# Dense products of a fused two-block transformer kernel: one plain fp32 matmul in place of three on split operands, and a ring of ten places

## The reference

```python
def first_block(...):            # 2 layers
    for l in range(DEPTH):
        mix = token_mixing(...)  # z = x @ w_in; pooled, sparse-attention and memory branches,
                                 # each times w_br, weighed by sigmoid(x @ w_gate), summed, @ w_out
        x = layer_norm(DN_ALPHA * x + mix, ln1_g[l], ln1_b[l])
        ffn = moe(...)           # 16 experts, 2 per token: (silu(x @ w1) * (x @ w3)) @ w2
        x = layer_norm(DN_ALPHA * x + ffn, ln2_g[l], ln2_b[l])

def _layer(...):                 # second block, 2 layers
    z = rms(x) @ w_in            # then window attention, forget-gate attention, mLSTM
    x = x + concat([ya, yb, yc]) @ w_out
    u = rms(x, norm2) @ w_ff1
    return x + square(relu(u)) @ w_ff2
```

## Time and profile before

| | |
|---|---|
| median of 3 executions | 2056.72 us (2053.87 to 2058.24) |
| the profiled execution's own time | 2056.15 us |
| its span, first to last instruction | 2053.5 us |
| PE busy | 1757.6 us |
| DVE busy | 773.7 us |
| ACT busy | 643.4 us |
| mean granted TensorE clock | 0.912 |

### The profile page before, as it was taken

One profiled execution on the slowest core, in us unless ns is written; L12 is line 12 of the kernel. 1 busy time (PEld: TensorE's weight loads), 2 busy tenths in 40 slices (PEclk: granted clock), 3 DMA queues, 4 the chain that ended last, 5 costly groups with the idle time before them and its releaser, 6 DMA issues.

```text
span 2053.5 us, 22089 instructions
## 1 busy us (share of the span) xinstructions
PE 1757.6 (86%) x9214; PEld 1290.8 (63%) x9214; DVE 773.7 (38%) x1476; ACT 643.4 (31%) x1041; POOL 29.5 (1%) x49
## 2 busy tenths in 40 slices
PE   5898987798897998987798895867899988588999
PEld 4768886443334777885443332855499977447997
DVE  3545443200104446343200103634255545525554
ACT  2425531110002435521110003443244443514442
POOL 4000000000000000000000000000000000000000
PEclk8999998799998999998799997875899999669999
DMA  8343445499997453445499995430155546003553
GB/s 237 98 144 118 139 153 203 148 387 386 386 387 244 124 163 107 142 163 186 153 386 386 387 386 201 147 123 0 41 185 185 186 136 199 13 21 103 191 189 112
DMA packets 233278, 392.67 MB, mean 191 GB/s; under 512 B 7124, under 2 KB 97280, under 8 KB 232784
## 3 DMA queue, kind: packets, MB, share of 16 engines
q1 hardware_dynamic: 229760, 380.30, 53.9%
q0 software_dynamic: 3264, 9.61, 1.5%
q10 hardware_dynamic: 144, 1.24, 0.2%
HBM read 390.07 MB, written 1.05 MB: 190 GB/s over the span
## 4 chain that ended last, share of the span: by engine, by line
PE 71%; DVE 9%; DMA 7%; SPq 6%; ACT 5%; issue 2%; DVEq 0%; ACTq 0%
PE psum L503 68%; SPq L2034 6%; DMA ring_sb<-in_w 4%; PE psum L629 2%; DMA ring_sb<-in_w_in 1%; ACT ring_rounded L1092 1%; DVE ring_rounded L1434 1%; DMA ring_sb<-in_w_out 1%; PE psum L548 1%; ACT region_sb L1118 1%; DVE x_sb L1545 0%; ACT xT_hi_rounded L1317 0%; DVE x_sb L1543 0%; DVE region_sb L1818 0%; DVE region_sb L1821 0%
## 5 line engine op out<-in xcount | busy, mean ns | idle before, releaser
L503 PE MATMUL psum<-ring_sb,region_sb 128*64 128x512 f32 (+1 forms) x1728 | 431.8, 602 | 44.3 <-DMA ring_sb<-in_w 34.5
L1434 DVE TENSOR_TENSOR ring_rounded<-ring_sb,ring_rounded 128x2048 fp32r<-128x2048 f32 (+4 forms) x152 | 321.5, 2130 | 259.0 <-ACT ring_rounded L1092 259.0
L503 PE MATMUL psum<-xT_hi_rounded,ring_rounded 128*128 128x256 f32 x1920 | 356.1, 287 | 0.0
L503 PEld LDWEIGHTS psum<-ring_sb,region_sb 128*64 128x64 f32 (+1 forms) x1728 | 151.5, 144 | 308.4 <-issue 289.6
L1092 ACT ACTIVATE ring_rounded<-ring_sb 128x2048 fp32r<-128x2048 f32 (+4 forms) x152 | 268.1, 1781 | 225.3 <-PE psum L503 143.2
L503 PE MATMUL psum<-ring_rounded,xT_hi_rounded 128*128 128x384 f32 (+4 forms) x960 | 280.1, 369 | 44.8 <-DVE ring_rounded L1434 25.2
L503 PE MATMUL psum<-xT_lo_rounded,ring_rounded 128*128 128x256 f32 x960 | 285.1, 297 | 28.3 <-DVE ring_rounded L1434 16.8
L503 PEld LDWEIGHTS psum<-xT_hi_rounded,ring_rounded 128*128 128x128 f32 x1920 | 306.7, 196 | 1.8 <-issue 0.5
L503 PEld LDWEIGHTS psum<-ring_rounded,xT_hi_rounded 128*128 128x128 f32 x960 | 185.8, 200 | 70.1 <-issue 45.2
L503 PEld LDWEIGHTS psum<-xT_lo_rounded,ring_rounded 128*128 128x128 f32 x960 | 189.0, 197 | 31.9 <-issue 18.1
L503 PE MATMUL psum<-ring_rounded,region_rounded 128*128 128x512 f32 x768 | 178.7, 392 | 3.0 <-DVE region_rounded L2020 3.0
(11 more groups left out here) (239 smaller groups left out, 1344.1 us busy)
## 6 DMA issues: line engine op xcount, KB each, us to landing
ring_sb<-in_w SPq DMA_DIRECT2D x192, 1024.0 KB, 14.2
ring_sb<-in_w_ff SPq DMA_DIRECT2D x64, 1024.0 KB, 5.3
ring_sb<-in_w_in SPq DMA_DIRECT2D x32, 1024.0 KB, 5.3
ring_sb<-in_w_in SPq DMA_DIRECT2D x24, 768.0 KB, 4.4
ring_sb<-in_w_out SPq DMA_DIRECT2D x16, 1024.0 KB, 5.2
ring_sb<-in_w_br SPq DMA_DIRECT2D x12, 1024.0 KB, 5.2
ring_sb<-in_w_mem_kv SPq DMA_DIRECT2D x8, 1024.0 KB, 5.1
ring_sb<-in_w_in SPq DMA_DIRECT2D x8, 904.0 KB, 4.8
```

The costliest lines, as they stand in the source:

```text
L503: return nc.tensor.matmul(dst, lhsT, rhs, start=first, stop=last, skip_group_check=True)
L1434: nc.vector.tensor_tensor(rounded(piece.raw), piece.raw, reread(piece.hi), ALU.subtract).then_inc(lo_made, 1)
```

## The change

Nothing is split any more. Each product is one matmul on plain fp32; the second places, both roundings, the split of the activations and their semaphores are gone. A piece takes one place, and the ring has ten. The turned x is copied out of PSUM half by ACT and half by DVE. The feed-forward's hidden rows are squared by one DVE instruction. The probabilities of the mLSTM heads move from the second half of the split x to the memory keys' and values' tiles. Each piece of w_out waits for single merged chunks in place of pairs.

```diff
-RING = 9
+RING = 10
...
-        def product(dst, lhsT, rhs, first, last):
-
-            if len(lhsT) == 2 and len(rhs) == 2:
-                (p, dp), (q, dq) = ([rounded(o) for o in both] for both in (lhsT, rhs))
-                matmul(dst, p, dq, first, False)
-                matmul(dst, dp, q, False, False)
-                return matmul(dst, p, q, False, last)
...
         def pe_wait_weights(piece):
-            if piece.split:
-                pe.wait_ge(lo_made, piece.split_count)
-            else:
-                pe.wait_ge(*piece.landed)
+            pe.wait_ge(*piece.landed)
...
-                        last = product(psum[:, i, 0:n], [o[:, k, b * P:(b + 1) * P] for o in lhs],
-                                       [w[:, c, :] for w in parts(piece)], k == 0, k == KC - 1 and bias is None)
+                        last = matmul(psum[:, i, 0:n], lhs[:, k, b * P:(b + 1) * P], piece.w[:, c, :],
+                                      k == 0, k == KC - 1 and bias is None)
...
-            pe_held(l, "mixed", xT, [merged_lo.at(l, c) for c in range(4)])
+            pe_held(l, "mixed", mergedT, [merged.at(l, 8 + k) for k in range(KC)])
...
-                if piece.split:
-                    a.wait_ge(*piece.landed)
-                    a.wait_ge(*ring.free_at(piece.position + 1))
-                    nc.scalar.activation(rounded(piece.hi), piece.raw, ACT.Copy).then_inc(hi_made, 1)
...
-                if piece.split:
-                    v.wait_ge(hi_made, piece.split_count)
-                    nc.vector.tensor_tensor(rounded(piece.raw), piece.raw, reread(piece.hi), ALU.subtract).then_inc(lo_made, 1)
...
         def vec_xT(l, phase):
...
+            for c in range(0, KC, 4):
+                i, full = loose.of(("xT", l, phase * 4 + 2 + c // 4))
+                v.wait_ge(*full)
+                nc.vector.tensor_copy(xT[:, c:c + 4, P:S], psum[:, i, :].rearrange("p (c t) -> p c t", c=4)).then_inc(xT_right.sem, 1)
...
-                    nc.vector.tensor_tensor(kept, kept, kept, ALU.mult).then_inc(relu_squared.sem, 1)
-                    v.wait_ge(*hidden_hi.at(l, n))
-                    nc.vector.tensor_tensor(rounded(hiddenT[j % 2][1][:, f, :]), kept, reread(hiddenT[j % 2][0][:, f, :]),
-                                            ALU.subtract).then_inc(hidden_lo.sem, 1)
...
+                    nc.vector.tensor_tensor(hiddenT[j % 2][:, f, :], upT[f % 2][:, :], upT[f % 2][:, :], ALU.mult).then_inc(hidden_made.sem, 1)
```

More of the change, by code:

```diff
@@ L175, in __init__ @@
         self.slots, self.loaded = slots, loaded
[L176 to L191, removed]
+        self.pieces, self.released = [], {}
+        for position, source in enumerate(plan):
+            turn, at = divmod(position, len(slots))
+            a, b = source.shape[1:]
+            view = slots[at][:, 0:a * b].rearrange("p (a b) -> p a b", a=a)
+            self.pieces.append(Piece(source, position, view, (loaded[at], 16 * (turn + 1))))
+        self.taken = self.started = 0
     def next(self):
@@ L204, in may_start @@
     def may_start(self):
[L205 to L208, removed]
+        return self.started < len(self.pieces) and (self.started < len(self.slots) or self.started - len(self.slots) in self.released)
 def by_rows(ap):
@@ L532, in used @@
                 ring.release(piece, (weights_used, used_count[0]))
-        n_split = 0
-        for piece in ring.pieces:
-            n_split += piece.split
-            piece.split_count = n_split
         def pe_turn(key, src, width, freed_by, *ready):
@@ L611, in pe_held @@
                             k = part_ * KC // 2 + c
-                            pe.wait_ge(*ready[k // 2])
-                            last = product(held[:, b, half * BANK:(half + 1) * BANK],
-                                           [o[:, k, b * P:(b + 1) * P] for o in lhs], [w[:, c, :] for w in parts(piece)],
-                                           k == 0, k == KC - 1)
+                            pe.wait_ge(*ready[k])
+                            last = matmul(held[:, b, half * BANK:(half + 1) * BANK], lhs[:, k, b * P:(b + 1) * P], piece.w[:, c, :],
+                                          k == 0, k == KC - 1)
                         if part_:
@@ L1072, in tensor_second @@
                             for f in range(4):
-                                last = product(held[:, b, half * BANK:(half + 1) * BANK], [h[:, f, b * P:(b + 1) * P] for h in hidden],
-                                               [w[:, f, :] for w in parts(piece)], j == 1 and f == 0, j == steps and f == 3)
+                                last = matmul(held[:, b, half * BANK:(half + 1) * BANK], hidden[:, f, b * P:(b + 1) * P], piece.w[:, f, :],
+                                              j == 1 and f == 0, j == steps and f == 3)
                             if j == steps:
@@ L1270, in scalar_mix @@
                 merge(2, dc)
-            round_hi(first + 42)
-            for c in range(4):
-                a.wait_ge(*merged.at(l, 8 + 2 * c + 1))
-                a.wait_ge(*dense.of(("branch", l, 2, 7))[1])
-                nc.scalar.activation(rounded(xT[0][:, 2 * c:2 * c + 2, :]), mergedT[:, 2 * c:2 * c + 2, :], ACT.Copy).then_inc(merged_hi.sem, 1)
             act_norm(l, 0)
@@ L1365, in scalar_second @@
             cut(1)
-            round_hi(first + 2 * 2 + 5)
             for n in range(4):
```

244 lines of the change are left out of this document (80 added, 164 removed).

## The result

The changed kernel takes 2118.74 us, the median of 4 executions (2116.92 to 2126.41), against 2056.20 (2053.87 to 2058.24) of the kernel before: ratio 1.0312, 95% interval 1.0283 to 1.034. It is slower by some 62 us. In a second set, run later, it took 2118.95. The profiled execution has a span of 2115.8 us, 62.3 more than the 2053.5 of before; the forecast was +74. The time, 2118.74, lies in the range of its likeliest case, 2110 to 2150, and 11 us under its middle, 2130.

The account below looks back on a forecast made before the run. PE was taken to bound the dense stages, the weight stream the expert stages. Dearer products +178.8 us, router +1.6, vanished waits and clock -106 make +74: 2056 becomes 2130 us, range 2104 to 2158.

Parts of the forecast that it names:

- likeliest case: Whole kernel: dearer products outweigh the vanished waits, 2130 us, own range 2110 to 2150, chance 0.80.
- The price of a product: All formerly split products: plain costs more at every width, +0.072 us at 256 to +0.177 at 512, sum +178.8 us.
- The 1750 us estimated from it: Whole kernel by the skill page's 131 ns: plain products at 0.52 us (512) and 0.26 (256), about -200 us.
- End of gates and w_out: First block, both layers: waits of 28.1 us and 9.8 us of lower clock go, gain 38.
- some 12 us earlier after the last merge began: Sign for the first block: w_out ends that much earlier, with no PE wait for anything near it.
- Feed-forward: Second block: entry waits (7.2 x 2), lower clock behind them (2.2 x 2) and a late hidden-rows wait go, gain 23.7 us.
- The tenth place: Expert stages: one more piece loaded beforehand saves one piece's time in each, gain 5.2 us for two.
- The second block's attention: Entry waits (5.6 and 1.7 us) and the head norms' 11.9 us wait go, gain 19.2 us.
- The start: First loads: all ten go out at once, cut 2 ends at about 59 us; net -8, gain 13.
- held by the DMA engines: Rival at the start: the DMA engines hold the loads, gain 3 us; part of the smaller-gains case, chance 0.08.
- The case of larger gains: DVE and ACT freed of roundings, so short attention waits may close too: 34 us more gain, 2096 us, chance 0.09.

Follow-up runs that it names:

- two kernels that differ in nothing else: Changed kernel with nine places, 2125.36 us; the same with three fp32r matmuls on a standing tile per formerly split product, 1954.71 us.
- the kernel with this edit alone: Kernel before, with only the first block's w_out in plain fp32 and its merged rows no longer split: 2027.38 us, ratio 0.9865.

## Why the forecast was right, and where it was off

The mechanism came out as forecast: dearer products at every place against waits that go, the first the larger. Its terms came out unequally, and three of them miss in ways that partly cancel.

**The price of a product: right.** It was read from steady starts and not from the mean in the groups, and it held at every width. The feed-forward stages show it pure: +82.1 between two kernels that differ in nothing else, 82.2 forecast. In the windows above a plain 512 product is two records of 0.429 us. The Trainium skill, "TensorE: Matmul & The Clock Gate", section Back-to-back issue gap, gives about 131 ns for a sustained matmul of 512 columns; the traces here do not agree, neither in these records nor in those of a split product, 0.227 us. The 1750 us estimated from it is out.

**End of gates and w_out: right.** Net of the dearer products it was forecast at 37.9 - 11.3 = 26.6; the kernel with this edit alone is 28.2 faster. The sign "some 12 us earlier after the last merge began" names the wrong merge, as the wait of 5.6 us stands in front of the last two: from there to the end of w_out it was 50.0 us before and is 38.0 now.

**Feed-forward: right.** +58.5 forecast, +59.2 measured; the entry waits are gone, and the clock column is 1.00 in the whole stage.

**The tenth place: right**, 5.2 against 5.7 in the two expert stages.

**The second block's attention: the term that was mis-sized.** The forecast took the bare waits, 7.3 us at the entries and 11.9 for the head norms in both layers, and no clock behind them, though it counted it at w_out and in the feed-forward. Idle time fell as forecast: 19.0 in both stages together, of 19.2. But PE's busy time at the lower clock fell there from 112.6 to 80.0 us too. From its first product to the wait for the decay keys (L1883) the first layer took 1356.37 - 1282.96 = 73.4 us before; with 13.0 for the dearer products that would be 86.4, and it takes 76.1: 10.3 gained where the wait is 6.0, so 4.3 of clock. Not all of that stands behind the head norms: of the 9.2 us of work at the lower clock in this stretch before, 4.8 stand ahead of their wait, behind the entry's, and 4.5 behind it (in the second layer 3.4 and 3.8); in the changed kernel there is none in either. Behind the next wait 1.4 more. Then there is a stretch of pure work behind the wait of 12.46 us that both kernels have. In windows, before and after, some 8 us behind its end:

```profile
1393.40:1400.40 7.00, 7.00 (x44) 5.77 (x44) 1.91 (x5) 1.11 (x4) 0.00 (x0) 0.51 0.01 2
```

```profile
1399.50:1406.40 6.90, 6.49 (x54) 4.96 (x54) 3.92 (x10) 3.37 (x8) 0.00 (x0) 1.00 0.00 1
```

PE is busy nearly throughout in both, at clock 0.51 in the one and 1.00 in the other; the stretch from that wait to the next long one takes 20.7 us before and 17.3 after. Together: 4.3 + 1.4 + 3.5 in the first layer and 3.4 + 1.2 + 0.5 in the second, 14 of the 15 us. The wait put back at the head norms shows 4.4 us of clock for a wait there in each layer. What the entry's waits gave back was not tested by itself, and that the 3.5 belong to the head norms was not shown either, for the fall inside the stretch did not return with their wait.

**The start: near the forecast, but not by its mechanism.** Net -8 was forecast, -5.7 measured. The first ten loads do not go out at once: the third is issued at 3.19 us and lands 32.27 later (the chain above), and the tenth is issued at 38.90. From 35.50 on PE works without a break and does not wait for the second piece of cut 2, as the forecast had it. Cut 2 then begins at 45.13, where the forecast had 45 for another reason, which is luck; it ends later than 59, since two bias products of 1.05 us each, left out of the sum, stand in it. So it is not the rival "held by the DMA engines", which left a gain of 3, either. One of its two bias products:

```profile
45.13 10.57 PE L465 MATMUL psum<-ring_sb,xT_sb 128*128 128x512 f32 x24
55.62 1.12 PE L465 MATMUL psum<-region_sb,consts_sb 1*128 1x512 f32 x2
```

PE's waits for the first loads of cut 0 and of cut 1 take 5.7 and 0.9 us in one profile and 5.4 and 2.0 in another, and the first mixing stage has 10.8 us of PE's busy time at the lower clock in the other, not 3.4. So this part varies between executions; the stage is 356.3 and 357.9 us long.

**The experts: a cost that was not in the sum.** The branch's wait in layer 1, 5.2 us. It was there in the trace of before, in layer 2 only (4.66 us of "issue" in front of the norm), and I had taken it for a fixed part of the code around it. Why the shorter program meets it in both layers is open, as said above.

So the error of 12 us is 15 too little for the clock in the attention, 3 in mixing, less 5 for the branch and 1 in the feed-forward. The case of larger gains was named for short waits in the attention that may close; the waits stayed, and it was the clock between them that rose. And "the sum of prices and gains" was itself a simplification: with the prices in place the gains are 20 us smaller (81 against 101), or, said the other way, with the gains in place the prices are 20 us larger (171 against 151). Both take work out of the same stretches at the lower clock: what the one has taken the other can't, as the 36.9 us above show. The forecast's 101 for the gains at nine places is the first of these numbers, and its 178.8 for the products is 8 more than the 171 measured.

## What to carry to other kernels

Compare a split product and a plain one by the steady interval of starts in a window of one kind, and count how many records each has; here three fp32r matmuls cost 0.36 us at 256 columns and 0.68 at 512, one plain fp32 product 0.43 and 0.86. What the preparation of operands costs is to be read from PE's waits, not from the busy time of the engines that do it: 650 us less of DVE and ACT together gave back, together with the longer products, 78 us of idle time and some 40 of clock. So change the operands only where they are late: w_out alone in plain fp32 and the roundings in a better order took 49 us from the kernel, the change at all places added 62. And price each vanished wait of some 6 to 10 us as the wait and some 2 to 4 us of clock behind it, then look whether a later stretch between waits keeps the higher level too.

## What the runs showed of the hardware

- The granted clock behind a wait of 7.8 to 10.4 us costs 2.3 to 2.7 us in a dense stream of products, and 4.4 behind one of 5.9 us in the attention, where other waits follow.
- In attention the clock can stay at 1.2 GHz through a stretch of 22.4 us with PE busy for 19.2 of them, and which stretch it is depends on the program: the same stage had 49.5 us of busy time at the lower level in one order of the roundings and 69.1 in another, though the wait for the head norms was shorter in the second (3.4 against 6.0 us).
- With nearly all waits in place (idle time 284.6 against 295.9 us), dearer products alone cut PE's busy time at the lower clock from 218.7 to 174.2 us.
- Behind a branch past skipped code DVE stood 4.7 to 5.6 us in three places with nothing to release it, with a 16 KB packet of an instruction queue in each, and 0.41 us in a fourth without one of that size. What decides between them was not shown.
